# Who splits the second chunk of the hybrid layer's in-projection weights

## What is computed

```python
h = layer_norm(DEEPNORM_ALPHA * h + squared_relu_mlp(h, w_up[layer], w_down[layer]),
               ln2_g[layer], ln2_b[layer])
...
proj = rmsnorm(x, norm1_gain) @ w_in        # w_in: 1024 x 1720
```

## Time and profile before

| what | value |
|---|---|
| time of three runs | 1506.03, 1508.97, 1510.93 us; median 1508.97 us |
| span of the profiled execution, first to last instruction | 1500.8 us |
| the profiled execution's own time | not listed beside the span; by the median, 8.2 us lie around the span |
| TensorE busy | 88% of the span |
| TensorE's mean granted clock | 0.953 of full speed |
| the stage of the change | about 656 to 717 us of the span |
| the twin stage | about 335 to 360 us |

### The profile page before, as it was taken

The page is one execution under the profiler, slowest core; times in us unless marked ns, Lnnn a source line. Parts: engine busy times, 40 slices in busy tenths (PEclk is TensorE's granted clock), DMA queues, the critical chain, the costliest instruction groups (busy, mean ns, idle before and its releaser), DMA issues.

```text
span 1500.8 us, 19390 instructions
## 1 busy us (share of the span) xinstructions
PE 1328.0 (88%) x6346; PEld 943.9 (63%) x6346; DVE 957.0 (64%) x2274; ACT 553.8 (37%) x1155; POOL 393.2 (26%) x389
## 2 busy tenths in 40 slices
PE   7997899998997999989699798879888978888878
PEld 5896799997986999978478543434343534334333
DVE  4585655556556555565795677676777777677765
ACT  3453544454554444444564222222221222222221
POOL 0103000000001000030553544444434444445440
PEclk9997999999998999999899899999999989999999
DMA  9624455645413755644510899999999999999997
GB/s 352 226 85 84 157 179 187 193 165 196 148 53 104 233 184 180 196 161 147 176 57 1 331 420 421 421 421 421 421 422 421 421 422 421 421 422 421 421 421 313
DMA packets 97389, 406.89 MB, mean 271 GB/s; under 512 B 6939, under 2 KB 44508, under 8 KB 60476
## 3 DMA queue, kind: packets, MB, share of 16 engines
q0 software_dynamic: 39552, 276.60, 45.2%
q1 hardware_dynamic: 57788, 129.66, 25.2%
HBM read 404.90 MB, written 1.07 MB: 271 GB/s over the span
## 4 chain that ended last, share of the span: by engine, by line
PE 33%; DMA 23%; issue 14%; DVE 13%; PEld 10%; POOL 3%; ACT 2%; DVEq 0%; SPq 0%; POOLq 0%; PEldq 0%; ACTq 0%
DMA ring<-in_peer_uv,prob 21%; PE ps L665 8%; PE ps L666 8%; PE ps L667 8%; PE ps L797 5%; PEld ps L665 3%; PEld ps L667 3%; PEld ps L666 3%; DMA uv_gain<-in_peer_uv,prob 2%; DVE w_low L1819 1%; POOL small L1593 1%; DMA ring<-in_v_a 1%; DVE ring L2486 1%; DVE prob L2362 1%; DVE prob L2350 1%
## 5 line engine op out<-in xcount | busy, mean ns | idle before, releaser
L1819 DVE TENSOR_TENSOR w_low<-ring,w_high 128x1024 fp32r<-128x1024 f32 x140 | 165.1, 1222 | 174.6 <-ACT w_high L1165 174.3
L1165 ACT ACTIVATE w_high<-ring 128x1024 fp32r<-128x1024 f32 x142 | 142.3, 1052 | 204.5 <-PE ps L667 204.5
L665 PE MATMUL ps<-hT_high,w_high 128*128 128x256 f32 x512 | 145.2, 284 | 0.3
L666 PE MATMUL ps<-hT_low,w_high 128*128 128x256 f32 x512 | 144.8, 283 | 0.0
L667 PE MATMUL ps<-hT_high,w_low 128*128 128x256 f32 x512 | 144.6, 282 | 0.0
L1414 ACT ACTIVATE prob<-prob 128x4 f32<-128x4 f32 (+2 forms) x67 | 13.8, 206 | 348.0 <-DVE prob L2486 348.0
L797 PE MATMUL ps<-arena_v,sco 128*128 128x512 f32 x256 | 123.2, 626 | 20.0 <-ACT sco L1402 20.0
L1402 ACT ACTIVATE sco<-const,prob 128x128 f32<-128x128 f32 x256 | 84.1, 392 | 150.8 <-DVE prob L2496 136.9
L797 PE MATMUL ps<-ring,sco 128*128 128x512 f32 x192 | 101.8, 681 | 33.6 <-ACT sco L1402 33.6
L797 PE MATMUL ps<-arena_u,sco 128*128 128x512 f32 x256 | 115.7, 601 | 8.6 <-ACT sco L1402 8.6
L2486 DVE CUSTOM_DVE_ANT_0 arena_v<-arena_v,nat 128x1024 f32<-128x1024 f32 x64 | 78.3, 1223 | 46.5 <-DMA arena_v<-in_peer_uv,prob 46.5
(11 more groups left out here) (451 smaller groups left out, 3098.9 us busy)
## 6 DMA issues: line engine op xcount, KB each, us to landing
ring<-in_w_up SPq DMA_DIRECT2D x32, 1024.0 KB, 5.5
ring<-in_w_down SPq DMA_DIRECT2D x32, 1024.0 KB, 4.8
qkring<-in_qk_a SPq DMA_DIRECT2D x8, 1024.0 KB, 5.7
qkring<-in_qk_b SPq DMA_DIRECT2D x8, 1024.0 KB, 4.9
ring<-in_peer_wq SPq DMA_DIRECT2D x8, 1024.0 KB
ring<-in_w_in SPq DMA_DIRECT2D x8, 860.0 KB, 5.2
ring<-in_v_a SPq DMA_DIRECT2D x4, 1024.0 KB, 13.0
ring<-in_w_out_a SPq DMA_DIRECT2D x4, 1024.0 KB, 13.9
```

The lines of the kernel that those rows point to most:

```text
L665: pe.matmul(dst, a[0], b[0], start=start, stop=False, skip_group_check=True)
L666: pe.matmul(dst, a[0], b[1], start=False, stop=False, skip_group_check=True)
L1165: sc.activation(w_split[pair][0][:, part], ring[:, slot, part], ACT.Copy)\
L1819: ve.tensor_tensor(w_split[pair][1][:, part], ring[:, slot, part], w_split[pair][0][:, part].bitcast(F32), ALU.subtract)\
```

## The change

Chunk 1 of `w_in` is split as the other chunks are: high by ScalarE, right after chunk 0 and before the layer norm; low by VectorE, its first half before tile 0's `take_tile_low` and its second half after it. GpSimd's six instructions and their waits go. The chunk's load raises `raw1_landed`, on which ScalarE waits, and no longer `w2_landed`.

```diff
@@ SP, the loads of w_in
-                     landed="w2_landed" if j == 1 else f"raw{slot}_landed")
+                     landed=f"raw{slot}_landed")
@@ ScalarE
             in_high(0)
+            in_high(1)
             layer_norm(by_tile=True)
             in_high(2, "w0_used")
@@ GpSimd
             po.wait_ge(sem("small_landed"), count.take("small_landed", 16 * N_SMALL))
-            po.wait_ge(sem("w2_landed"), count.take("w2_landed", 16))
-            halves = [slice(0, D), slice(D, C_END)]
-            for part in halves:
-                po.tensor_scalar(ring[:, 1, part], ring[:, 1, part], gain1_turned[:, 1:2], None, ALU.mult)\
-                    .then_inc(sem("rope_step"), 1)
-            for part in halves:
-                po.wait_ge(sem("rope_step"), count.take("rope_step"))
-                po.tensor_copy(w_in_pairs[1][0][:, part], ring[:, 1, part]).then_inc(sem("rope_step"), 1)
-            po.wait_ge(sem("rope_step"), count.take("rope_step", 2))
             layer_norm((0,))
-            for part in halves:
-                po.tensor_tensor(w_in_pairs[1][1][:, part], ring[:, 1, part], w_in_pairs[1][0][:, part].bitcast(F32),
-                                 ALU.subtract).then_inc(sem("w2_split"), 1)
             layer_norm((1,))
@@ VectorE
-            def in_low(c):
+            def in_low(c, halves=range(2)):
 
                 high, low = w_in_pairs[w_in_place[c]]
-                for a, z in ((0, D), (D, C_END)):
+                for half in halves:
+                    a, z = ((0, D), (D, C_END))[half]
                     ve.wait_ge(sem("w_high"), count.take("w_high"))
@@ VectorE
             in_low(0)
-            layer_norm_by_tile(3, meanwhile=[lambda: take_tile_low(0)])
+            layer_norm_by_tile(3, meanwhile=[lambda: in_low(1, (0,)), lambda: take_tile_low(0), lambda: in_low(1, (1,))])
             ve.sem_inc(sem("norm_due"), 2)
             in_low(2)
```

## The result

The kernel after takes 1498.86 us (median of 20 runs, 1496.31 to 1507.18), the kernel before 1508.37 us (20 runs, 1501.53 to 1511.43). The ratio is 0.995 with a 95% interval of 0.9938 to 0.9963: 7.5 us faster, between 5.6 and 9.4. Forecast were 1504.4 us and a range down to 1501.8, so the time lies outside the range; the sign was right and the size was not. Two later comparisons of the same two kernels gave 0.9927 (0.9915 to 0.994) and 0.996 (0.9938 to 0.9982), which is 11.0 and 6.0 us: the gain is clear of noise, its size is known to a few us only.

What follows compares the result with a forecast made beforehand. TensorE was taken to bound the kernel, waiting on tile 0's norm behind GpSimd's work. Chunk 2 starting at 677.24, not 681.78, saves 4.54 us: span 1496.3 plus 8.2 gives 1504.4 us, range 1501.8 to 1508.2.

Steps and rivals of the forecast that it cites:

- GpSimd's late answer: Tile 0's norm: GpSimd starts its norm work only behind its own casts, so VectorE's scaling starts 2.07 us late.
- the stretched scaling: Tile 0's norm: VectorE's scaling takes 3.29 us beside GpSimd's subtraction instead of 1.28, so 2.01 us to gain.
- the twin stage: Stage with the same norm and GpSimd free; its times, plus 320.84 us, gave the forecast positions.
- ScalarE's cover: ScalarE's two added high instructions, 1.90 us, end at 661.51, before the row sum due at 661.78: cost nothing, 0.27 us spare.
- rival (d): Ahead of the norm: ScalarE waits for a late chunk load, up to 3.2 us slower, 1512.2 us; chance 0.04.
- VectorE's added first half: Before tile 0's eviction: low's first half runs until 669.74, costs 0.5 us; chunk 0 still starts 3.38 us earlier.
- VectorE's chain: Tile 1's norm and chunk 2's low part on VectorE, no longer TensorE, set chunk 2's start at 677.24.
- Rival (a): Behind tile 0's transposes: the clock falls again, chunk 2 starts at 678.40, 3.4 us gained, 1505.6 us; chance 0.12.
- (b): Tile 0's scaling is stretched by the moment's loads, not GpSimd: 2.01 us stay, 2.5 gained, 1506.4 us; chance 0.08.
- (e): Stage of the change: low clock lasted longer in typical executions before, 5.5 us gained, 1503.5 us; chance 0.12.
- all later work follows it: Behind chunk 2's first product: all later work only shifts with its start, so the whole 4.54 us is kept.
- 8.2 us lie around the span: Median 1508.97 less profiled span 1500.8, added to the forecast span of 1496.3 to give 1504.4 us.

Runs made afterwards that it cites:

- a_sub2: Kernel after with GpSimd's two subtractions put back as idle work on a buffer nobody needs, between its parts of the two norms: 1501.89 us, ratio 0.9969.
- b_same: The kernel before, unchanged, run again for a second profile: 1506.85 us, ratio 0.9978 against the same kernel.
- b_look: The kernel before, unchanged, run again for a third profile: 1506.08 us, ratio 1.0001 against the same kernel.
- a_subwarm: Kernel after with GpSimd's two idle subtractions and 8 extra matmuls in TensorE's idle time before tile 0's transposes: 1502.19 us.
- a_late19: Kernel after with 19 useless matmuls (4.4 us) on TensorE behind chunk 2's products for tile 0: 1502.90 us.
- a_late10: Kernel after with 10 useless matmuls (2.3 us) on TensorE behind chunk 2's products for tile 0: 1503.59 us.
- a_late15: Kernel after with 15 useless matmuls (3.45 us) on TensorE behind chunk 2's products for tile 0: 1504.25 us.
- b_order: Kernel before with GpSimd keeping the whole split but doing its part of tile 0's norm ahead of its two casts: 1499.76 us, ratio 0.9939.
- a_fill: Kernel after with both halves of chunk 1's low part moved behind VectorE's centring of tile 1: 1500.16 us, ratio 0.995.
- a_fill2: Kernel after with only the second half of chunk 1's low part moved behind VectorE's centring of tile 1: 1499.85 us, ratio 0.9935.

## Why the prediction was right and wrong

*Right, step by step.* GpSimd's late answer and the stretched scaling were the two costs in the stage, and the twin stage priced them: scaling of tile 0 from 11.87 to 10.03 us behind the first matmul (forecast 9.80) and from 3.29 to 1.29 us. ScalarE's cover held: `in_high(1)` ended 0.33 us before the row sum needed it, and rival (d) didn't come. VectorE's added first half set the start of chunk 0, and VectorE's chain the start of chunk 2, as written. Rival (a) didn't come, (b) fell with a_sub2, and (e) with b_same and b_look. The 0.2 us missing are GpSimd's: its root of tile 0 started at 9.36, in the twin at 9.14.

*Right in kind, too small.* A fall of the clock in the new schedule was priced by rival (a) at 678.40 - 677.24 = 1.16 us. Between a_sub2 and a_subwarm it is worth 24.38 - 22.72 = 1.66 us. This did not change the sum, which rests on positions at the full clock.

*Wrong.* The step that failed is the assumption that "all later work follows it": the sum has no term for any stage behind chunk 2. The attention stage took 87.4 and 87.5 us in b_same and b_look and 81.0 to 81.5 us in the three profiles of after. With it goes the reading that 8.2 us lie around the span. The profiled executions with a known time leave 1.8 to 2.0 us around theirs (1498.77 - 1497.0; 1508.55 - 1506.7). So the profiled execution of before took about 1502.6 us, an estimate from its span, 6 us below the median: it had an attention stage of 81.4 us. I read a median 6 us above the profile as a constant and added it on both sides. With 1.8 us in place of 8.2, the forecast span of 1496.3 gives 1498.1 us, close to the 1498.77 of the profiled execution of after.

How much of the surplus the whole set of executions owes to this stage is an estimate. If all 114 of 148 executions of before above 1505 us had the long stage, and the five of 32 of after, 6 us each make 3.7 us; with the stage's 4.34 that is 8.0 us, against 7.5 by the ratio, 11.0 and 6.0 in the later comparisons, and 9.5 between the medians. The times of before are too spread for such a clean split, so the agreement supports this account and doesn't prove it.

*The page that spoke for it.* The Trainium skill, "TensorE: Matmul & The Clock Gate", Part 1, says that the point at which the clock changes is run-variable. I used it for the stage of the change alone, where it was to make up to 2 us more or 1 us less; three profiles of before show 0.1 us there (25.44, 25.53, 25.55). The clock does differ between these profiles further back, from 755 us on, in a stage that no part of the change touches.

*What stays open.* Why the change makes the long attention stage rarer. It moved the start of that stage 4.3 us forward, but the distance from the start to the clock's fall grew only from 1.9 to 2.1 us to 2.6 to 2.9 us, and no run shows what sets this distance: a_late19 has 2.1 us more work ahead of the stage than a_late10, yet its fall comes 2.0 us behind the start and not earlier than the 1.42 us of a_late10. Open too are how the fall at 720 us and the low stretch from 755 us on are linked, and where the unprofiled executions of a_late15, from 1500.69 to 1509.7 us, lost their time; its profile is the fastest of its twelve.

## What to carry to other kernels

Look for bulk work queued ahead of a tiny step on the critical path. Here moving GpSimd's two norm instructions ahead of its casts gave 85% of the stage's gain (3.70 of 4.34 us) without giving its work to other engines. Before a profile is taken as the median, its own time has to be known, which is its span and a small constant (1.8 us here). If the median lies further off, the profile is not of a typical execution, and a second and a third one are needed. Where TensorE's clock changes inside a later stage, as much as the gain can be won or lost there (6.4 us here between b_same and after), so price a change in its stage by positions, and say of the total only what several executions show.

## What the hardware showed that was not expected

Two executions of one kernel, before and b_same, agree to 0.1 us in the stage of the change and are 6.0 us apart in the attention stage, with the same instructions. From 760 to 770 us the clock is 1.00 in the first and 0.50 in the second, where TensorE is busy 5.00 of each 5 us.

VectorE's scaling was stretched by 2.0, 1.5 and 0.7 us beside a GpSimd subtraction (before), an idle subtraction (a_sub2) and a cast (b_order). It goes the other way too: GpSimd's root on 128x1, 0.55 us in after, took 1.48 and 1.13 us in a_fill and a_fill2, where VectorE's low part had started 0.23 us ahead of it. One case doesn't fit: VectorE's centring of tile 0 in before, with two SBUF inputs too, took 1.29 us at 664.27, although GpSimd's scaling ran until 664.92 and a cast from 664.87. Spans on GpSimd are rough, so this stays open.
